# A float32 transformer block on one core: both feed-forward products in seven half-size block products each

## The reference

```python
h  = h + mixer_layer(h, ...)                 # ends with merged @ w_out
hn = rms_norm(h, mlp_norm_g)                 # [1024, 1024]
h  = h + square(relu(hn @ w_up)) @ w_down    # w_up [1024, 4096], w_down [4096, 1024]
```

## Time and profile before

| what | value |
|---|---|
| median of 3 runs | 1851.68 us |
| the profiled execution's span | 1847.9 us |
| TensorE busy | 1818.2 us (98%) |
| VectorE / ScalarE / GpSimd busy | 766.3 / 575.1 / 85.0 us |
| mean granted TensorE clock | 0.999 |
| moved by DMA | 124.41 MB, 67 GB/s over the span |

### The profile page before, as it was taken

How to read it: one execution, slowest core, us unless ns; L and a number is a source line. 1 busy time by engine, 2 the same in 40 slices (tenths; PEclk the granted TensorE clock), 3 DMA queues, 4 the chain that set the end, 5 groups by cost and what they waited for, 6 DMA issues and landing times.

```text
span 1847.9 us, 24330 instructions
## 1 busy us (share of the span) xinstructions
PE 1818.2 (98%) x8888; PEld 1501.9 (81%) x8888; DVE 766.3 (41%) x1520; ACT 575.1 (31%) x1239; POOL 85.0 (5%) x153
## 2 busy tenths in 40 slices
PE   7999999999999999999999999999999999999999
PEld 6777888888788888888887887888888878887887
DVE  4211355422556576755564335332332233222321
ACT  5322345333445454543222134321231123112310
POOL 1000001100000000002221000000000000000000
PEclk9999999999999999999999999999999999999999
DMA  5111122211102020204553111111111111111112
GB/s 181 46 46 48 53 86 89 99 46 46 52 27 78 26 71 26 72 27 157 180 194 126 63 46 46 46 46 46 46 46 46 46 47 46 46 50 43 46 59 101
DMA packets 56274, 124.41 MB, mean 67 GB/s; under 512 B 7153, under 2 KB 7217, under 8 KB 56177
## 3 DMA queue, kind: packets, MB, share of 16 engines
q1 hardware_dynamic: 42912, 78.66, 13.2%
q0 software_dynamic: 13264, 44.44, 7.0%
HBM read 101.94 MB, written 20.97 MB: 67 GB/s over the span
## 4 chain that ended last, share of the span: by engine, by line
PE 91%; DMA 3%; DVE 3%; ACT 2%; issue 1%; SPq 0%; DVEq 0%; ACTq 0%
PE bank L446 26%; PE bank L451 26%; PE bank L450 26%; PE bank L709 4%; DVE WL L1162 2%; PE bank L670 2%; PE bank L703 1%; DMA RAW<-in_w_in 1%; PE bank L689 1%; PE bank L691 1%; DMA RAW<-in_w_down 1%; DMA RAW<-in_w_up 1%; ACT WH L844 1%; PE bank L626 1%; DMA RAW<-in_w_out 0%
## 5 line engine op out<-in xcount | busy, mean ns | idle before, releaser
L446 PE MATMUL bank<-HN,WH 128*128 128x512 f32 x896 | 358.6, 400 | 3.7 <-DVE WL L1162 3.5
L450 PE MATMUL bank<-HN,WL 128*128 128x512 f32 x896 | 350.2, 391 | 6.7 <-issue 6.7
L451 PE MATMUL bank<-HN,WH 128*128 128x512 f32 x896 | 350.7, 391 | 0.0
L844 ACT CAST WH<-RAW 128x512 fp32r<-128x512 f32 x280 | 167.6, 621 | 378.2 <-PE bank L451 278.2
L1162 DVE TENSOR_TENSOR WL<-RAW,WH 128x512 fp32r<-128x512 f32 x280 | 184.7, 689 | 199.7 <-ACT WH L844 198.8
L451 PEld LDWEIGHTS bank<-HN,WH 128*128 128x128 f32 x896 | 168.6, 188 | 43.6 <-issue 7.1
L446 PEld LDWEIGHTS bank<-HN,WH 128*128 128x128 f32 x896 | 168.8, 188 | 40.1 <-DVE WL L1162 7.7
L446 PE MATMUL bank<-WH,UH 128*128 128x512 f32 x512 | 199.9, 390 | 0.9 <-DVE WL L1162 0.8
L450 PE MATMUL bank<-WH,UL 128*128 128x512 f32 x512 | 199.3, 389 | 0.0
L451 PE MATMUL bank<-WL,UH 128*128 128x512 f32 x512 | 199.2, 389 | 0.0
L450 PEld LDWEIGHTS bank<-HN,WL 128*128 128x128 f32 x896 | 169.0, 189 | 31.0
(11 more groups left out here) (211 smaller groups left out, 2442.4 us busy)
## 6 DMA issues: line engine op xcount, KB each, us to landing
RAW<-in_w_in SPq DMA_DIRECT2D x104, 256.0 KB, 2.9
RAW<-in_w_up SPq DMA_DIRECT2D x64, 256.0 KB, 3.2
RAW<-in_w_down SPq DMA_DIRECT2D x64, 256.0 KB, 3.3
gates<-TB POOLq DMA_DIRECT2D x48, 256.0 KB, 2.3
TH<-gates POOLq DMA_DIRECT2D x32, 256.0 KB, 3.0
y_raw<-RT POOLq DMA_DIRECT2D x8, 512.0 KB, 3.1
RAW<-in_w_swa_branch SPq DMA_DIRECT2D x16, 256.0 KB, 3.1
YB<-y_raw POOLq DMA_DIRECT2D x8, 512.0 KB, 4.1
```

The lines of the kernel that those rows point to most:

```text
L446: mm = pe.matmul(bank, ahi, bhi, start=first, stop=False)
L450: pe.matmul(bank, alo, bhi, start=False, stop=False)
L451: return pe.matmul(bank, ahi, blo, start=False, stop=last)
L844: act.copy(WH[:, k, :], RAW[:, k % 4, :]).then_inc(w_hi, 1)
```

## The change

Both products are done by Strassen's scheme in Winograd's form. `hn` is cut into four blocks of 512 features by 512 tokens, `w_up` into pairs of 128-column strips with two halves of depth, `w_down` likewise; each product of 2 by 2 blocks becomes seven block products of half size, with sums of blocks as operands and of results.

- **First product.** 16 pairs of strips f, seven products t each: 12 matmuls a product (4 k-tiles by 3), 7 x 16 x 12 = 1344 in place of 1536. For each pair SyncE loads 1 MB of `w_up` (`WRAW`, 1 KB rows); VectorE makes four sums of its blocks (`XS`); ScalarE and VectorE split seven operands into `WH`/`WL`, which are now a ring of eight, eight products ahead (`up_hi`, `up_lo`). The moving operands are `A11`, `A12`, `A22` (contiguous) and four sums in `SOP`, whose columns lie in runs of 128. Of the seven products three open a bank and four add onto one after ScalarE or VectorE has taken its earlier value: two banks for each f, in turn for even and odd f. ScalarE and VectorE make the four blocks of `U` from them (copies, adds, relu, square) and VectorE four sums (`US`); GpSimd stores all seven, 256 KB each, to `uop` in DRAM.
- **Preparing `hn`** (`hop_hi`, `hop_lo`). The transposes of block b-1 stand after block b. Blocks 0 to 3 are only split (and copied to `RA`); for blocks 4 to 7 ScalarE and VectorE also make the four sums, one of them on GpSimd (`sum_s4`), and split each. GpSimd stores `H1` to DRAM, since its place is used in between.
- **Second product.** Seven products t, each over 16 k-tiles into four banks: 7 x 16 x 12 = 1344 matmuls. In each step of 12, SyncE has loaded one 256 KB operand from `uop`; it is split into `ADH`/`ADL` (ring of four), and a `w_down` block or a sum of blocks into `WH`/`WL`. The blocks of `w_down` come in the first two products (SyncE and GpSimd), one of them twice. VectorE adds the banks to `H1` (`take_down`).
- All of it is written out, with no loop.

The core of the diff:

```diff
+UP_ORDER = [(0, 0), (0, 1), (1, 0), (1, 1)] + [(0, t) for t in range(2, 7)] + [(1, t) for t in range(2, 7)] \
+    + [(f, t) for f in range(2, UF) for t in range(7)]
 sync:
+                sp.dma_start(WRAW[f % 2][:, :, :],
+                             w_up[:, 2 * P * f:2 * P * (f + 1)].rearrange("(k p) n -> p k n", p=P))\
...
+                        sp.dma_start(XB[:, k, :], down(k, 0, 0)).then_inc(xb_full[k % 2], 16)
...
+                    if n >= 4:
+                        sp.wait_ge(da_ready, n - 3)
+                    sp.dma_start(ARAW[:, n % 4, :], uop[t, k]).then_inc(da_raw[n % 4], 16)
 gpsimd:
+                pool.dma_start(h1s[b], H1[:, b, :]).then_inc(h1_st[b // 4], 16)
+                if b >= 5:
+                    sum_s4(b - 1)
...
+                pool.wait_ge(da_ready, k + 2)
+                pool.dma_start(YB2[:, k, :], down(k, 0, 1)).then_inc(yb2_full[k % 4], 16)
+                if k % 4 == 1:
+                    pool.dma_start(H1[:, k // 4, :], h1s[k // 4]).then_inc(h1_ld, 16)
 tensor, up_product(f, t):
+                elif t == 2:
+                    pe.wait_ge(r1_rdy, f + 1)
+                elif t == 3:
+                    pe.wait_ge(c11_rdy, f + 1)
+                elif t == 4:
+                    pe.wait_ge(r2_rdy, f + 1)
...
+                pe.wait_ge(uw_ready, q + 1)
+                for k in range(4):
+                    mm = three(bank[:, :], WH[:, q % WS, ks], WL[:, q % WS, ks], *UP_OPS[t](k),
+                               t in (0, 1, 3) and k == 0, k == 3, False, t not in (0, 1, 3))
...
+            for f, t in UP_ORDER:
+                up_product(f, t)
+                if (f, t) == (0, 0):
+                    transpose_h(NB - 1)
 scalar, hop_hi(b) for b >= 4:
+                act.copy(R22[:, :, :], tile).then_inc(r22_rdy, 1)
+                act.copy(A22[:, 0, :, cols], tile).then_inc(h22_rdy, 1)
+                for n, i in enumerate((0, 1, 2, 3)):
+                    act.wait_ge((s1_rdy, s2_rdy, s3_rdy, s4_rdy)[i], b - 3)
+                    act.copy(sop_block(0, i, b), sum_src(i, cols)).then_inc(sop_hi, 1)
 scalar, per product q:
+                if t == 0:
+                    act.copy(R1T[f % 2][:, :], a_bank[:, :]).then_inc(r1_rdy, 1)
+                elif t == 2:
+                    act.copy(R2T[:, :], a_bank[:, :]).then_inc(r2_rdy, 1)
...
+                if q + WS < UN:
+                    up_hi(q + WS)
 vector, hop_lo(b) for b >= 4:
+                dve.tensor_tensor(S1B[:, :, :], tiles[0], R22[:, :, :], ALU.subtract).then_inc(s1_rdy, 1)
+                dve.tensor_tensor(R22[:, :, :], RA[:, 0, :, cols], tiles[0], ALU.subtract).then_inc(s3_rdy, 1)
+                dve.tensor_tensor(RA[:, 0, :, cols], S1B[:, :, :], RA[:, 0, :, cols], ALU.subtract).then_inc(s2_rdy, 1)
+                dve.tensor_tensor(A22[:, 1, :, cols], tiles[1], A22[:, 0, :, cols].bitcast(F32), ALU.subtract)\
+                for i in range(4):
+                    dve.wait_ge(sop_hi, 4 * (b - 4) + i + 1)
+                    dve.tensor_tensor(sop_block(1, i, b), sum_src(i, cols), sop_block(0, i, b).bitcast(F32),
+                                      ALU.subtract).then_inc(hop_rdy, 1)
```

More of the change, by code:

```diff
@@ L322, in _ @@
+            for f in range(4):
+                sp.wait_ge(dn_ev, 24 + f + 1)
+                sp.dma_start(out[(f + 4) * P:(f + 5) * P, 0:SL], H1[:, f + 4, 0:SL]).then_inc(last_done, 16)
+            sp.wait_ge(last_done, LD0 + 64)
+            sp.wait_ge(out_done, 16 * 12)
         @block.gpsimd
@@ L829, in _, with plain_op, sum_op, at_k @@
-            mlp(0)
-            with pe.Fori(1, FF_GROUPS) as g:
-                mlp(g)
+                    if c == 1 and b >= 1:
+                        transpose_h(b - 1)
+            def plain_op(pair):
+                return lambda k: (pair[:, 0, k, :], pair[:, 1, k, :])
+            def sum_op(i):
+                def at_k(k):
+                    hi, lo = (part[:, 4 * (i // 2) + k, :].rearrange("p (j r c) -> p j r c", j=4, r=2)[:, :, i % 2, :]
+                              for part in SOP)
+                    return hi, lo
+                return at_k
@@ L1574, in _ @@
                     j = DVE_F + 8 * c + b
-                    if c == 1 and b >= 2:
-                        lo_h(b - 2)
                     if b == NB - 1:
-                        next_lo(SLAB_F + c + 1, KT)
+                        if c == 0:
+                            next_lo(SLAB_F + 1, KT)
+                        else:
+                            for q in range(4):
+                                up_lo(q)
                     if c == 0:
@@ L1611, in _ @@
-            mlp(0, False)
-            with dve.Fori(1, FF_GROUPS - 1) as g:
-                mlp(g, False)
-            mlp(FF_GROUPS - 1, True)
+                        if b >= 1:
+                            hop_lo(b - 1)
+            up_sums(4)
+            up_lo(4)
+            hop_lo(NB - 1)
+            for q in range(5, WS):
+                up_sums(q)
+                up_lo(q)
+            for q, (f, t) in enumerate(UP_ORDER):
+                a_bank, c_bank = B[f % 2], B[6 + f % 2]
+                if t in (1, 4, 5):
+                    dve.wait_ge(up_mm, q + 1)
+                if t == 1:
+                    dve.wait_ge(r1_rdy, f + 1)
+                    dve.tensor_tensor(R1T[f % 2][:, :], c_bank[:, :], R1T[f % 2][:, :], ALU.add).then_inc(c11_rdy, 1)
+                elif t == 4:
+                    dve.wait_ge(r3_rdy, f + 1)
+                    dve.tensor_tensor(R3T[:, :], R3T[:, :], a_bank[:, :], ALU.subtract).then_inc(c22_rdy, 1)
+                elif t == 5:
+                    dve.wait_ge(r2_rdy, f + 1)
+                    dve.tensor_tensor(R2T[:, :], c_bank[:, :], R2T[:, :], ALU.subtract).then_inc(c12_rdy, 1)
+                if q + WS < UN:
+                    up_sums(q + WS)
+                if f >= 2 and t == 0:
+                    u_sums_a(f - 1)
+                elif f >= 2 and t == 1:
+                    u_sums_b(f - 1)
+                elif f == 1 and t == 2:
+                    u_sums_a(0)
+                    u_sums_b(0)
+                if q + WS < UN:
+                    up_lo(q + WS)
@@ new lines, in _, with down_sum @@
+            u_sums_a(UF - 1)
+            u_sums_b(UF - 1)
+            def down_sum(t, k):
+                n = UF * t + k
+                if t == 2:
+                    dve.wait_ge(zb_full[k % 4], ZB0 + 16 * (k // 4 + 1))
+                    dve.wait_ge(x1_add, k + 1)
+                if t == 6:
+                    dve.wait_ge(z_add, k + 1)
+                dve.tensor_tensor(XT[:, n % 4, :], (YB2 if t == 4 else XB)[:, k, :], ZB[:, k, :], ALU.add)\
+                   .then_inc(xt_rdy, 1)
@@ L1617 @@
+            for f in range(4):
+                take_down(6, f)
 _INS = ["x", "meta_tokens", "mix_norm_g", "w_in", "ret_norm_g", "q_norm_g", "k_norm_g", "sinks",
```

467 lines of the change are left out of this document (362 added, 105 removed).

## The result

The changed kernel takes **1775.92 us** in the median of four runs (1775.26 to 1776.17) against 1850.78 for the kernel before on the same chip (1849.67 to 1854.08): ratio 0.9591, interval 0.9577 to 0.9604, 4.1% less. The prediction was 1779.0, in the range 1758 to 1815. The profiled execution has a span of 1774.6 us, 1.0 under the 1775.6 that the terms of the prediction add up to.

The account below looks back on a forecast made before the run. TensorE, busy for 98% of the span, was taken as the bound. From 1847.9, -99.2 gave 1748.7; +18.9, +7.5 and +0.5 gave a span of 1775.6, and 3.8 for the median offset made 1779 us, range 1758 to 1815.

Parts of the forecast that it names:

- (a): Both products: 2688 matmuls of the same shape in place of 3072, 384 fewer at 0.2268 us each, -87.1.
- (b): TensorE's two loop jumps back lose 3.59 and 3.55 us, and half clock after the second 1.6; without a loop, -8.7.
- (c): First slab after w_out: 3.4 us of waits for weights in the kernel before go, -3.4; the rebuilt place is priced separately.
- preparing hn: After w_out, VectorE's 9.0 us rounds lag TensorE's 6.36; four waits of 5.2, 2.8, 7.3 and 3.6, +18.9.
- turn: Start of the second product: operands are split only after the first product's last bank; 5.9 wait plus 1.6 half clock, +7.5.
- end: End of the kernel: as before, but four stores instead of two lie close together, +0.5.
- end of w_out: Taken as unmoved on TensorE; the prediction called itself wrong if w_out's end moves.
- The sum on GpSimd: Preparing hn: priced at nothing; may last 1.9 before VectorE waits; ends 0.69 (nothing) and 2.8 (+3.6), skill estimate 1.35.
- The rival of steady costs: Steady hand-overs cost 0.1 to 0.25 us per product, 22 to 56, giving 1793 to 1840; chance 0.12.
- Steady parts at nothing: Steady stretches of both products: the other engines' work fits beside TensorE's 2.72 us per product, so no cost.
- The rival of engines in turn: ScalarE and VectorE alternate instead of overlapping: +73 in the first product, +85 in the second, 1937; chance 0.05.
- DMA at nothing: Second product's first two block products need 337 GB/s; rows show 252 and 410; taken nothing, upper end +21; rival's chance 0.08.

Follow-up runs that it names:

- experiment 2: Changed kernel with product seven's 12 matmuls repeated into an unread bank in each of the 16 steps of f: 1819.57 us.
- experiment 3: Changed kernel without the sums of activation blocks and their splits; products three to six multiply A22: 1757.74 us.
- experiment 4: Changed kernel, but VectorE splits the sums of block b-2 between H1(b) and norm_h(b), where it stood idle: 1772.68 us.
- experiment 7: Changed kernel with the idle-gap split, reordered queues at hn, and w_out's second half taking heavy and light blocks by turns: 1769.53 us.
- experiment 10: Changed kernel, but VectorE makes the fourth sum (S4) in place of GpSimd: 1777.00 us.
- experiment 1: Changed kernel with the splits of the second product's first two steps ahead of the last relus, squares and sums: 1767.48 us.
- experiment 5: Changed kernel with VectorE repeating weight splits twice more in the first product and splits of U's rows once in the second: 1812.07 us.
- experiment 9: Changed kernel with reordered queues and blocks, early splits at the turn, and later weights prepared four products ahead until f = 2: 1754.29 us.
- experiment 6: Changed kernel with the idle-gap split and four more moves in the queues of ScalarE, VectorE and TensorE where hn is prepared: 1771.93 us.

## Why the prediction was right

Point by point, in the prediction's own steps; the sum against the profiled span of before, 1847.9:

| step | predicted | measured |
|---|---|---|
| (a) 384 matmuls | -87.1 | -87.1 (first product by experiment 2: 192 are worth 43.65; second by the list of waits alone) |
| (b) loop jumps and the clock behind | -8.7 | -8.7, none left |
| small waits of before, not named | 0 | -4.1 |
| (c) first slab | -3.4 | -3.4 |
| preparing hn | +18.9 | +20.9 |
| turn | +7.5 | +8.0 |
| end | +0.5 | +0.1 |
| end of w_out | 0 | +1.3 |
| span | 1775.6 | 1847.9 - 73.0 = 1774.9, and 1774.6 read |

- **What goes** was right in (a) and (b). It was short by 4.1 us: from 1129.88 on the prediction counted 16.2 us of waiting (714.7 less 696.7 and 1.76) but named only 12.1 of it (8.7 and 3.4). The rest were waits of 0.1 to 0.5 us for weights at the starts of slabs, from 1181 us on; the changed kernel has none after 1170.44 but the turn. This is the step with an error in it: a remainder was left unassigned, and so was costed as if it stayed.
- **Preparing hn** was right in its mechanism: a round of VectorE of 9.42 (predicted 9.0) against 6.36 of TensorE, shown by experiments 3, 4, 7 and 10. The four waits were forecast as 5.2, 2.8, 7.3 and 3.6 and are 5.35, 1.03, 7.95 and 1.50. The two short ones are smaller because the products in front of them ran at half clock, which the prediction had said takes the place of waiting there. Product seven starts 38.9 after the end of w_out (37.0 predicted). What it mis-sized is the round: the first split of sums is 0.47 longer beside GpSimd's sum, and 0.15 passes before it. Four rounds of 0.42 are 1.7 of the 1.9 by which product seven is late (an estimate from these rows).
- **The sum on GpSimd** lasts 1.28, between the bounds 0.69 and 2.8, and is not waited for by VectorE's last split of a round, as priced. The estimate 1.35 from the Trainium skill (GPSIMD Engine Reference, 3.1) was near. That it would stretch VectorE's operation was not priced.
- **The turn** was right in cause and size; experiment 1 takes away all but 0.4 of it.
- **The rival of steady costs** is given as 1793 to 1840; its own 22 to 56 us make 1801 to 1835. Nothing hangs on it.
- **Steady parts at nothing** was right. Experiment 2 shows it for the first product, and in the list of waits nothing recurs. The rival of engines in turn is excluded by experiment 5.
- **DMA at nothing** was right at the nearer of its two rows: 350 GB/s of these blocks of 256 KB for 43 us, and TensorE without a gap. The Trainium skill (DMA: Bandwidth & Descriptors, Bandwidth) has 341 GB/s at 1 MB and less for smaller transfers; here the measurement differs and decides. Two readings on the way were off. The 410 GB/s row was not one of 256 KB blocks alone: 1.13 of its 1.64 MB came by GpSimd's queue, which loads x in 512 KB transfers. And two block products of 14.7 MB are 29.4, not 27.3, so the upper end was +30 and not +21. The sign "DMA at its full share" came half true, without a wait behind it: 99%, where the prediction had counted on a reserve.
- **Strided columns at nothing** was right: 0.2267 per matmul on SOP.
- **The end** was 0.4 less than predicted. The profiled execution's span lies 1.3 under the median where 3.8 were taken, so 2.5 of the 3.1 us between forecast and result come from that offset and not from the kernel. The offset was misread: every execution of the result and the experiments takes 1.5 to 1.6 longer than its span, so the rest of the 3.8, some 2 us, comes from the kernel before having been profiled in one of its quicker executions (an estimate).
- **The end of w_out**, 1.3 later, was named as a sign of being wrong, but is no effect of the change: w_out starts 1.45 later already (1037.62 and 1036.17), behind the same instructions of TensorE, and the kernels of the experiments have its end anywhere from 1128.87 on.

The errors are of both signs: 4.1 too little taken off and 0.4 too much for the end on one side, 2.0 too little for hn, 0.5 too little for the turn and the 1.3 ahead of w_out on the other. That the sum fits within 1 us is luck; its terms are good to some 2 to 4 us.

## What to carry to other kernels

Where one engine is full and the others have room, work taken off it is won at its full price in the steady part, and the question is only what happens at the ends: here 73 of a possible 103 us arrived, and nearly all the rest was lost in two short places, of 40 and 8 us, where a new preparation stood in one queue. Such a place is to be read as a race of rounds (VectorE 9.4, TensorE 6.4, times the heavy rounds in a row) and then as queues: a copy that frees a bank belongs in front of casts that are due later. When an earlier event brings little, look for the next wait a few products on before calling the bound: experiments 4, 6 and 7 won about 3 us or less each, and experiment 9, which freed R2T, collected most of the rest (together with the turn the whole way from 1775.9 to 1754.3, below the kernel that makes no sums at all, which still has the turn).

## What the runs showed of the hardware that was not expected

- A VectorE split with both operands in SBUF lasts 1.14 to 1.18 us in place of 0.68 while GpSimd adds a 128x512 tile (1.28 us); it does so in every round and no longer when GpSimd's sum is gone (experiment 10). It is not that split's own: where another operation with both operands in SBUF stands beside the sum, that one is long (a split of weights in experiments 7 and 9, 1.15 and 1.14). VectorE's split in front of it, which reads a bank, runs beside the same sum at 0.68. The Trainium skill (SBUF — State Buffer, Who interferes with whom) says that the two share a port pair as an exclusive lock; the trace agrees in the main: the split, begun while the sum still had 0.61 to run, ends 0.55 after it (1126.39 and 1125.84), a little less than the 0.68 that it lasts alone.
- A VectorE operation on 128x512 in a row of independent ones costs 0.605, not its length of 0.69 (experiment 5: 32 of them and three waits of 0.76 in 21.45). The prediction read the pitch as 0.62 from four in 2.49; the distances in that row are (2.49 - 0.69) / 3 = 0.60.
- The granted clock fell to 0.50 after waits of 5.35, 7.95 and 5.58 us and not after those of 1.03 and 1.50; the distance of 0.427 also stood behind waits of 2.06 and 2.92 us in experiments 1 and 4. In experiment 1 the turn without its wait kept 1.00, so there a wait of 5.74 cost 8.0. Where another wait follows close behind, the half clock cost nothing: product one ran 12 matmuls at half clock in experiment 1 and about seven in the changed kernel, and block 7's transposes start 12.5 after the end of w_out in both.
